# Moving loads and a small transpose to other places in an eight-core encoder layer

## What is computed

```
h += 0.5*SwiGLU_1(RMSNorm(h, g_ffn1))              # D 2048, DFF 5632
z  = RMSNorm(h, g_mix) @ w_in                      # q,k,v of 16 heads of 128, and 8 forget logits
o_A (heads 0..7)  = attention over 64-row chunks, 9 chunks of keys, + rel_bias[clipped distance]
o_B (heads 8..15) = causal attention, + F[t]-F[s], F = cumsum(log_sigmoid(z_f + b_forget))
h += concat(o_A, o_B) @ w_out
h += 0.5*SwiGLU_2(RMSNorm(h, g_ffn2))
h += sigmoid(RMSNorm(h, g_ple) @ w_ple_gate) * (p @ w_ple_proj)     # p has 256 columns
out = RMSNorm(h, g_final)
```

## Time and profile before

| what | us |
|---|---|
| four timed runs | 4741.4, 4731.5, 4568.0, 5091.8 |
| their median | 4736.5 |
| the profiled execution, its own time | 4562.2 |
| its span, slowest core (core 6) | 4560.6 |
| spans of the eight cores | 4530.5 to 4560.6 |

### The profile page before, as it was taken

The page is one execution under the profiler, slowest core; times in us unless marked ns, Lnnn a source line. Parts: engine busy times, 40 slices in busy tenths (PEclk is TensorE's granted clock), DMA queues, the critical chain, the costliest instruction groups (busy, mean ns, idle before and its releaser), DMA issues.

```text
span 4560.6 us, 50711 instructions; the slowest of 8 cores (4530.5 to 4560.6 us)
## 1 busy us (share of the span) xinstructions
PE 4073.3 (89%) x19000; PEld 1776.8 (39%) x19000; DVE 1412.1 (31%) x1835; ACT 712.5 (16%) x1032; POOL 225.9 (5%) x217
## 2 busy tenths in 40 slices
PE   4999999995997999999998996798879999999977
PEld 2434433442453344344333443244233344344333
DVE  2232233223013322322341102543533322332344
ACT  3000000003003000000021002476030000000034
POOL 0000000000001000000000000000000000000000
PEclk9999999997998999999998997899989999999988
DMA  8664665535638445635516553421465435635243
GB/s 159 73 85 56 74 77 72 64 48 113 114 70 113 72 63 70 90 56 74 74 19 100 112 114 111 151 68 45 83 81 78 73 56 74 93 56 73 39 72 95
DMA packets 444765, 365.89 MB, mean 80 GB/s; under 512 B 86384, under 2 KB 399984, under 8 KB 440560
## 3 DMA queue, kind: packets, MB, share of 16 engines
q0 software_dynamic: 371504, 267.47, 43.2%
q1 hardware_dynamic: 73024, 95.18, 6.6%
HBM read 600.71 MB, written 29.36 MB: 138 GB/s over the span
## 4 chain that ended last, share of the span: by engine, by line
PE 82%; DVE 6%; DMA 4%; issue 4%; ACT 2%; SPq 1%; DVEq 0%; POOL 0%; another core or an unknown queue 0%; ACTq 0%; POOLq 0%
PE pf L331 20%; PE pf L420 20%; PE pf L415 20%; PE pf L491 7%; PE pf L507 5%; DVE H_u L336 4%; PE pf L838 2%; SPq L143 1%; PE pf L721 1%; PE pf L718 1%; PE pf L679 1%; ACT xn_u L280 1%; DMA win_u<-w_in 1%; PE pf L691 1%; DMA gbc_u<-gains 1%
## 5 line engine op out<-in xcount | busy, mean ns | idle before, releaser
L331 PE MATMUL pf<-wd_u,aT_u 128*128 128x512 bf16 x4224 | 1020.9, 378 | 114.9 <-DVE H_u L336 62.1
L415 PE MATMUL pf<-xnT_u,wgu_u 128*128 128x512 bf16 x4224 | 958.6, 380 | 13.4 <-DMA wgu_u<-w2gu 13.4
L420 PE MATMUL pf<-xnT_u,wgu_u 128*128 128x512 bf16 x4224 | 954.7, 379 | 2.2 <-DMA wgu_u<-w2gu 2.2
L336 DVE SCALAR_TENSOR_TENSOR H_u<-pf,H_u 128x512 f32<-128x512 f32 x1184 | 818.6, 692 | 430.5 <-PE pf L331 388.7
L428 DVE TENSOR_TENSOR aT_u<-pf,sg_u 128x512 bf16<-128x512 f32 x264 | 182.6, 692 | 1671.6 <-PE pf L420 1671.6
L331 PEld LDWEIGHTS pf<-wd_u,aT_u 128*128 128x128 bf16 x4224 | 350.4, 96 | 778.4 <-issue 514.4
L415 PEld LDWEIGHTS pf<-xnT_u,wgu_u 128*128 128x128 bf16 x4224 | 414.2, 98 | 514.2 <-issue 18.7
L420 PEld LDWEIGHTS pf<-xnT_u,wgu_u 128*128 128x128 bf16 x4224 | 413.2, 98 | 500.8 <-issue 2.7
L425 ACT ACTIVATE sg_u<-pf 128x512 f32<-128x512 f32 x264 | 157.6, 597 | 2655.3 <-PE pf L415 2655.3
L491 PE MATMUL pf<-xnT_u,win_u 128*128 128x512 bf16 x1536 | 338.2, 384 | 56.8 <-DMA win_u<-w_in 56.8
L491 PEld LDWEIGHTS pf<-xnT_u,win_u 128*128 128x128 bf16 x1536 | 151.5, 99 | 242.7 <-issue 65.6
(11 more groups left out here) (91 smaller groups left out, 1575.1 us busy)
## 6 DMA issues: line engine op xcount, KB each, us to landing
wgu_u<-w1gu POOLq DMA_DIRECT2D x84, 1024.0 KB, 15.0
wd_u<-w1d POOLq DMA_DIRECT2D x22, 2048.0 KB, 27.7
wgu_u<-w2gu POOLq DMA_DIRECT2D x42, 1024.0 KB, 10.7
win_u<-w_in POOLq DMA_DIRECT2D x18, 2048.0 KB, 16.4
wd_u<-w2d POOLq DMA_DIRECT2D x11, 2048.0 KB, 19.6
bmf_u<-rb_toep SPq DMA_DIRECT2D x64, 256.0 KB, 4.7
H_u<-x_prev SPq DMA_DIRECT2D x8, 1024.0 KB, 20.6
H_u<-x_own SPq DMA_DIRECT2D x8, 1024.0 KB, 18.4
```

Source lines behind the costliest of these rows:

```text
L331: k.op(k.pe, lambda t=t, cg=cg, jl=jl, bank=bank: nc.tensor.matmul(pf[bank][:, :], lhsT=act_aps[jl][:, t * 128:(t + 1) * 128], rhs=wd_slot ...
L336: k.op(k.dve, lambda t=t, cg=cg, bank=bank: nc.vector.scalar_tensor_tensor(out=H[:, t, cg * 512:(cg + 1) * 512], in0=pf[bank][:, :], scala ...
L415: k.op(k.pe, lambda c=c, s=s, jj=jj, tg=tg, bg=bg: nc.tensor.matmul(pf[bg][:, :], lhsT=wgu[s][:, c, jj * 128:(jj + 1) * 128], rhs=xnT[:, c ...
L420: k.op(k.pe, lambda c=c, s=s, jj=jj, tg=tg, bu=bu: nc.tensor.matmul(pf[bu][:, :], lhsT=wgu[s][:, c, 256 + jj * 128:256 + (jj + 1) * 128], ...
```

## The change

It edits five places and nothing that is computed.

1. At the start the gain is loaded ahead of the 8 tiles of `H` instead of behind them.
2. `inproj` asks for `wf` when block 1 begins, behind the load of block 2, and not ahead of block 0. In the first call the 8 loads of `x_own` into `H` are issued there too, and not ahead of `inproj(0)`.
3. The p stage stands ahead of the sel8 stage, in the same scope and without a barrier of its own; it writes `pb[1]` instead of `pb[0]`.
4. `load_head` issues the 8 loads of `bmf` ahead of the 5 loads of q, k and v.
5. `load_g(0)` loads the first `wg` as four DMAs of 512 KB with a tile each, and the matmuls wait for the quarter that they read.

```diff
@@ ffn
-                    load_gain(entry_gain)
+                    if entry_gain >= 0:
+                        load_gain(entry_gain)
@@ inproj(which, after_first=None)
-                with nc.allow_non_contiguous_dma(reason="tiny forget-gate weight columns"):
-                    k.dma(k.pool, wf[:], w_in[:, 6144:6152].rearrange("(c p) n -> p c n", p=128), t_wf)
                 load_blk(0)
...
                     if i + 1 < len(blocks):
                         load_blk(i + 1)
+                    if i == 1:
+                        with nc.allow_non_contiguous_dma(reason="tiny forget-gate weight columns"):
+                            k.dma(k.pool, wf[:], w_in[:, 6144:6152].rearrange("(c p) n -> p c n", p=128), t_wf)
+                        if after_first is not None:
+                            after_first()
@@ the order of the stages
+        load_gain(0)
         load_H(x_prev)
-        ffn(w1gu, w1d, 1, entry_gain=0)
-        load_H(x_own)
-        inproj(0)
+        ffn(w1gu, w1d, 1, entry_gain=-1)
+        inproj(0, after_first=lambda: load_H(x_own))
         ffn(w1gu, w1d, 1, entry_gain=0)
         inproj(1)
+        pT = sb("pT", [128, 2, NTOK], BF16)
         with ExitStack() as fx:
...
+            for t in range(NT):
+                i = t % 2
+                k.dma(k.sp, pf32[i][:], p_own[t * 128:(t + 1) * 128, :], t_p32[i])
+                k.op(k.dve, lambda i=i: nc.vector.tensor_copy(out=pbf[i][:], in_=pf32[i][:]), reads=[t_p32[i]],
+                     writes=[t_pbf[i]])
+                for c in range(2):
+                    k.op(k.pe, lambda c=c, i=i: nc.tensor.transpose(out=pb[1][:, c, :],
...
+                         reads=[t_pbf[i], t_id], writes=[tpb[1]], inc=(c == 1))
+                k.op(k.act, lambda t=t: nc.scalar.copy(out=pT[:, :, t * 128:(t + 1) * 128], in_=pb[1][:, 0:2, :]),
+                     reads=[tpb[1]], writes=[t_pT])
             sel8_d = SEL8_D
@@ load_head
+                        if h < 8:
+                            for di in range(8):
+                                k.dma(k.sp, bmf[:, di, :], rb_toep[h, di], t_bmf[di])
                         k.dma(k.sp, qT[s][:], s_qT[h], t_hd[s][0])
...
-                        if h < 8:
-                            for di in range(8):
-                                k.dma(k.sp, bmf[:, di, :], rb_toep[h, di], t_bmf[di])
@@ behind attention
-        pT = sb("pT", [128, 2, NTOK], BF16)
...
-            k.barrier()
-
@@ load_g
+                if cb == 0:
+                    for qq in range(4):
+                        k.dma(k.pool, wg[s][:, qq * 4:(qq + 1) * 4, :], src[:, qq * 4:(qq + 1) * 4, :], t_wg[s][qq])
+                else:
+                    k.dma(k.pool, wg[s][:], src, t_wg[s][0], extra=t_wg[s][1:])
```

More of the change, by code:

```diff
@@ L435, in ffn, with inproj @@
                 k.barrier()
-        def inproj(which):
+        def inproj(which, after_first=None):
             with ExitStack() as s2:
@@ L547, in load_H @@
                 k.dma(k.sp, H[:, t, :], src[t * 128:(t + 1) * 128, :], tH[t])
+        load_gain(0)
         load_H(x_prev)
-        ffn(w1gu, w1d, 1, entry_gain=0)
-        load_H(x_own)
-        inproj(0)
+        ffn(w1gu, w1d, 1, entry_gain=-1)
+        inproj(0, after_first=lambda: load_H(x_own))
         ffn(w1gu, w1d, 1, entry_gain=0)
         inproj(1)
+        pT = sb("pT", [128, 2, NTOK], BF16)
+        t_pT = T("pT")
         with ExitStack() as fx:
+            pf32 = [fx.enter_context(nc.sbuf_tensor(uq(f"pf32_{i}"), [128, DPLE], F32)) for i in range(2)]
+            pbf = [fx.enter_context(nc.sbuf_tensor(uq(f"pbf_{i}"), [128, DPLE], BF16)) for i in range(2)]
+            t_p32 = [T("p32a"), T("p32b")]
+            t_pbf = [T("pbfa"), T("pbfb")]
+            for t in range(NT):
[5 more added lines that the diff above has]
+                    k.op(k.pe, lambda c=c, i=i: nc.tensor.transpose(out=pb[1][:, c, :],
+                                                                   in_=pbf[i][:, c * 128:(c + 1) * 128],
+                                                                   identity=ident[:]),
+                         reads=[t_pbf[i], t_id], writes=[tpb[1]], inc=(c == 1))
+                k.op(k.act, lambda t=t: nc.scalar.copy(out=pT[:, :, t * 128:(t + 1) * 128], in_=pb[1][:, 0:2, :]),
+                     reads=[tpb[1]], writes=[t_pT])
             sel8_d = SEL8_D
@@ L801, in build @@
             wg = [s2.enter_context(nc.sbuf_tensor(uq(f"wg{i}"), [128, NC_, 512], BF16)) for i in range(2)]
-            t_wg = [T(f"wg{i}") for i in range(2)]
+            t_wg = [[T(f"wg{i}_{q}") for q in range(4)] for i in range(2)]
             wp = [s2.enter_context(nc.sbuf_tensor(uq(f"wp{i}"), [128, 2, 512], BF16)) for i in range(2)]
@@ L820, in load_g @@
                 s = cb % 2
-                k.dma(k.pool, wg[s][:], w_pg[:, cb * 512:(cb + 1) * 512].rearrange("(c p) n -> p c n", p=128),
-                      t_wg[s])
+                src = w_pg[:, cb * 512:(cb + 1) * 512].rearrange("(c p) n -> p c n", p=128)
+                if cb == 0:
[3 more added lines that the diff above has]
+                    k.dma(k.pool, wg[s][:], src, t_wg[s][0], extra=t_wg[s][1:])
                 k.dma(k.pool, wp[s][:], w_pp[:, cb * 512:(cb + 1) * 512].rearrange("(c p) n -> p c n", p=128),
@@ L839, in build @@
                             pf[bg][:, :], lhsT=xnT[:, c, t * 128:(t + 1) * 128], rhs=wg[s][:, c, :],
-                            start=(c == 0), stop=(c == NC_ - 1)), reads=[t_wg[s], tX[t]], writes=[tpf[bg]],
+                            start=(c == 0), stop=(c == NC_ - 1)), reads=[t_wg[s][c // 4], tX[t]], writes=[tpf[bg]],
                             inc=(c == NC_ - 1))
```

## The result

| | us |
|---|---|
| after, median of 7 runs (lowest 4466.4) | 4472.5 |
| before, median of 10 runs (lowest 4566.8) | 4653.4 |
| ratio after / before, 95% interval | 0.978 (0.977 to 0.980) |
| after, the profiled execution: its own time, its span (core 5) | 4466.4, 4464.9 |

The change is faster by 2.2%. Some executions of either kernel are longer, with a lower granted clock on the cores of one die or of both; the medians hold them, the ratio leaves them out. Between the two profiled executions the difference is 4562.2 - 4466.4 = 95.8 us, where the sum said 113.9: 84% of it came.

The account below looks back on a forecast made before the run. PE bounds the kernel (89% busy, 82% of the chain), so only its waits can be won: 20.5 + 26.1 + 4.4 + 5.7 + 53.7 + 3.5 = 113.9 us off 4562.2 gives 4448; range 4405 to 4640.

Parts of the forecast that it names:

- Attention: Group A heads: with `bmf` loaded first, 14.3 us a head; 53.7 us less in all, bounds 30.7 and 57.4.
- the start: Start of the kernel: with the gain loaded first, PE starts at 54.7 us, 20.5 less, bounds 12 and 22.
- so I take 35, a stall of 7.4: `inproj(0)`: block 2's weights land 35 us after issue, against 27.6 us of block 1's matmuls, so PE stalls 7.4.
- a stall over 15: `inproj(0)`: a stall over 15 us there was named as a sign that the prediction is wrong.
- the second rival: `inproj(0)`: `H` starves block 2's weights, no progress for 31 us, a stall of 19 instead of 7.4; 4460, chance 0.08.
- the old stall before block 1: `inproj(0)`: the wait of 3.9 us before block 1 goes, as `H` no longer delays it.
- That the stores are covered: `inproj(0)`: block 1's stores wait behind `H` until about 33 us after its begin, covered by the 7.4 us stall.
- The term was 4.4 in each stage: `inproj(0)` and `inproj(1)`: moving `wf` behind block 2 shortens each first wait by 4.4 us, bounds 1.2 and 5.5.
- The rival of 17.6: Attention, group A: the single-buffered bias load becomes the bound, 17.6 us a head, costing 23 us; 4471, chance 0.14.
- the one by which q, k and v become late: Attention, group A: `bmf` loads hold back q, k, v, the period stays near 21 us; 4498, chance 0.13.
- The p stage: Moved ahead of sel8: saves 19.15 us behind attention, `sel8f` load 13.4 later; net 5.7 less, bounds 3 and 8.
- the loss that the prediction's estimate by that page would give: Gate stage: four `wg` pieces one after the other take 12.8 us against 6.8 for one, a loss of some 6.

## Why the prediction was right, and where it wasn't

The predicted time was 4448 us, the measured one 4472.5. Attention and the start came out nearly as forecast. Two steps failed: the time that the sum was subtracted from, and the stall in front of block 2.

**The base: the first step that failed** is "The sum is made against the profiled execution's own 4562.2 us". On that base 4448 is 2.5% less, and against it the 2.2% measured is a miss of 18 us. But the median of before that was known was 4736.5, and 4448 is 6.1% under that one: 174 of these 288 us are in no term of the sum. What was measured is 2.2%: the gain that the terms stand for, not 6.1%. The prediction saw the gap and used it for its range, where it has 4623, but not for its time.

**`inproj(0)`: the second step that failed** is "so I take 35, a stall of 7.4". The weights landed after 43.7 to 48.2 us and the stall was 13.8 to 20.4, mean 17.0; a stall over 15 is one of the signs of being wrong that the prediction names. The step went from 24 us (as many packets as `wf`) up to 35 by feel. The bytes were there to be counted: 8.4 MB of `x_own` and 2.1 MB of weights at the 249 GB/s of the earlier trace rows are 42 us. This is the second rival in place and size (a stall of 19, 4460) and in its mechanism, `x_own` taking the bandwidth, though its "no progress" is too strong: the weights' queue moved 0.95 MB in the first 34 us. Two smaller misses stand in the same term: the wait before the first matmul came out at a mean of 12.6 and not 9.5, and the old stall before block 1 stayed (3.00 on the slowest core, 3.87 before). Together the term was 7.2 and not 26.1, below the bound of 15.

That the stores are covered was right as a fact (the cast waited 26.98 us) and as a judgement in this kernel: four staging tiles gave 0.6 us. That they are a cause of their own the prediction did not see; with 2 KB rows they alone made 20 us.

**`wf`.** The term was 4.4 in each stage; it was 1.6 and 2.2 by the waits with `wf` in front. By the ends of the two stages it was 2.8 and 2.0. The lower bound of 1.2 was its issue, and the measurement lies nearer to it than to 4.4: the earlier trace rows gave landing times of two transfers that overlapped, and their difference is not what the first delays the second by.

**The start** was right to 0.3 us, by its own steps: the first tile 3.2 us later (3.5 forecast), DVE at 20.42 (20.6), PE at 54.48 (54.7). It was kept downstream.

**Attention** was right in mechanism, and close in size: 14.0 us a head in the mean of the cores and 14.3 on the slowest, where 14.3 was taken from three limits that lay within a microsecond. The 2.1 us that the sum adds for the start of head 0 at the lower clock have no row; the seven heads took 98.3 us in the mean, where the sum has 102.2. Alone it gave 5.6 to head 0, 50.4 over the seven heads and 1.2 behind, 57.2 in all for 53.7. The seven periods were forecast from PE's 13.8 and the chain of one `bmf` buffer; which of the two sets the period now was not taken apart, but PE is busy for 92% of it and DVE still waits up to 3.2 us for `bmf`. The rival of 17.6 is out, as no period of any core is over 16.0, and so is the one by which q, k and v become late, as behind head 0 PE waits 1.6 us or less for them on any core.

**The p stage.** Net 4.0 for 5.7. It costs 11.3 in front of attention, where 13.4 was forecast: `sel8f` is 10.2 us behind the first load of `p`, since most of these loads land 1.9 to 2.4 us after their issue there, and on the slowest core of before they took 3.1 to 4.0. It saves 15.3 behind (19.15 forecast; that was the slowest core's, and four others had only 13.2 to 13.5). The slowest core of one execution was taken for all.

**The gate stage** gave 3.9 for 3.5. The Trainium skill, page "DMA: Bandwidth & Descriptors", section "Rules for kernel authors", asks for 1 MiB or more per DMA where the most bandwidth is wanted. The four of 512 KB had landed 15.4 us after the first was issued, the one of 2 MB after 15.6, so the split cost no time here, and the loss that the prediction's estimate by that page would give did not come.

**Who gets the bandwidth.** The same page's section "Queues, rings and completion order" has the engines take turns between queues packet by packet. The traces agree more closely than the earlier trace rows did: in the same 34 us, 1207 packets of SP's queue went beside 927 of POOL's with 8 KB rows, and 2744 beside 2047 with 2 KB rows. With `x_own`'s rows a quarter as large the weights came 10 us sooner.

## What to carry to other kernels

A load that is moved off the path must be put where its bytes fit beside what is already due there: sum both, divide by a rate that a window of the same profile shows, and hold that against the time to the next deadline; if it doesn't fit, spread it over the stages that have room. That sum tells when both are there, not which is first: with 2 KB rows the weights were there after 33 to 39 us and `x_own` after 43 to 52. When two waits lie on one another, lifting the shorter gives nothing and lifting the longer gives at most the difference, and an edit meant for one can lengthen the other, so test them together as well. Say against which time of the kernel before a sum is made, and give the forecast against that same time. And read a stage's cost over all cores before it is taken from one.

## What I had not expected

- A queue issue can be the slow part: SP took 25.5 us to issue four loads of 1024 rows of 2 KB, nearly all of it for the third and the fourth, while eight of 128 rows of 8 KB took 5.0.
- Starving goes both ways. Large plain packets held the weights back to 47 us from 16; a casting load of 4 MB held a plain load of 256 KB back to 26 us from 5.
- Cores differ in pairs. Before `inproj`'s first matmul, cores 0, 3, 5 and 6 of after wait 14.0 to 14.4 us in the first call and the others 9.8 to 11.8; in the second 12.6 to 13.4 against 8.9 to 9.2. One of each two neighbours is the late one in nearly every run looked at, though not always the same; with `x_own` in front the cores were closest (36.6 to 38.6 us). What they share was not tried.
